# Skipping unused expert slots and moving expert choice, last down weights and result scatter in a one-core hybrid decoder layer

## The reference, cut to what matters

```python
x = layer_norm(DEEPNORM_ALPHA * x + mix, ln1_g, ln1_b)            # x1, (1024, 1024)
aff = sigmoid(x2 @ router_w)                                      # (1024, 32)
sel = aff + router_bias
grp_score = top_k(sel.reshape(N, 4, 8), 2)[0].sum(-1)
top_grp = argmax(grp_score, axis=-1)
_, idx = top_k(where(in_grp, sel, -inf), 2)                       # two experts of the best group
w_sel = take_along_axis(aff, idx, axis=-1)
gate = w_sel / sum(w_sel)
# each expert e, in blocks of 128 tokens:
h = silu(xblk @ w_gate[e]) * (xblk @ w_up[e])                     # 1024 x 512 each
y = h @ w_down[e]                                                 # 512 x 1024
x = layer_norm(DEEPNORM_ALPHA * x + sum of the two y * gate, ln2_g, ln2_b)
```

## Time and profile before

| | us |
|---|---|
| median of 3 runs | 2498.57 |
| lowest and highest | 2492.93, 2500.19 |
| the profiled execution | 2487.82 |
| its span, first to last instruction | 2486.0 |
| PE busy | 2225.8 (90%) |
| DVE busy | 1279.5 (51%) |
| ACT busy | 890.7 (36%) |
| POOL busy | 577.1 (23%) |
| granted TensorE clock, mean | 0.953 of full speed |

### The profile page before, as it was taken

How to read it: one execution, slowest core, us unless ns; L and a number is a source line. 1 busy time by engine, 2 the same in 40 slices (tenths; PEclk the granted TensorE clock), 3 DMA queues, 4 the chain that set the end, 5 groups by cost and what they waited for, 6 DMA issues and landing times. The chain is left out here.

```text
span 2486.0 us, 31375 instructions
## 1 busy us (share of the span) xinstructions
PE 2225.8 (90%) x12070; PEld 1789.7 (72%) x12071; DVE 1279.5 (51%) x1347; ACT 890.7 (36%) x846; POOL 577.1 (23%) x405
## 2 busy tenths in 40 slices
PE   6999799997899998989979889989489999999985
PEld 5667577774687787878867767868377877787762
DVE  2567421115130565236657701245578888888855
ACT  2653111114011343102224312011257777777753
POOL 2223211101240000424536522400011222121202
PEclk8999899999999999999989989989599999999998
DMA  3245423323531431422323231131389999999975
GB/s 119 88 138 166 149 80 101 96 56 106 198 119 37 112 78 33 154 101 94 110 81 105 87 110 43 60 121 68 135 315 387 394 391 383 389 406 378 390 306 211
DMA packets 125374, 428.48 MB, mean 172 GB/s; under 512 B 33424, under 2 KB 54800, under 8 KB 112352
## 3 DMA queue, kind: packets, MB, share of 16 engines
q1 hardware_dynamic: 106544, 354.29, 40.5%
q10 hardware_dynamic: 9136, 38.80, 3.9%
q0 software_dynamic: 9600, 34.08, 3.7%
HBM read 351.44 MB, written 75.69 MB: 172 GB/s over the span
## 5 line engine op out<-in xcount | busy, mean ns | idle before, releaser
L3045 DVE TENSOR_TENSOR ex_sb_low<-landed,high 128x4096 fp32r<-128x4096 f32 x96 | 424.6, 4424 | 121.6 <-ACT high L2986 117.1
L2986 ACT CAST high<-landed 128x4096 fp32r<-128x4096 f32 x93 | 337.7, 3632 | 114.7 <-DMA landed<-exp_gate 63.7
L2902 POOL COPY ex_sb_idx<-slot_token 128x1 uint32 x30 | 62.2, 2072 | 409.0 <-PE ex_ps_x L2924 409.0
L160 PE MATMUL ex_ps_g<-high,ex_sb_xt 128*128 128x512 f32 x256 | 105.8, 413 | 10.3 <-DVE ex_sb_xt L3040 10.2
L160 PE MATMUL ex_ps_y<-high,ex_sb_ht 128*128 128x512 f32 x256 | 104.3, 407 | 9.8 <-DVE ex_sb_ht L3057 9.8
L161 PE MATMUL ex_ps_g<-ex_sb_low,ex_sb_xt 128*128 128x512 f32 x256 | 102.8, 402 | 0.0
L1087 DVE TENSOR_TENSOR rc_sb_ab<-rc_ps_m,mats 128x512 f32<-128x512 f32 x32 | 20.6, 686 | 159.7 <-PE rc_ps_m L970 159.7
L162 PE MATMUL ex_ps_g<-high,ex_sb_xt 128*128 128x512 f32 x256 | 102.7, 401 | 0.0
L160 PE MATMUL ex_ps_u<-high,ex_sb_xt 128*128 128x512 f32 x256 | 101.3, 396 | 1.1 <-DVE ex_sb_low L3045 1.1
L161 PE MATMUL ex_ps_y<-ex_sb_low,ex_sb_ht 128*128 128x512 f32 x256 | 101.5, 396 | 0.0
L162 PE MATMUL ex_ps_y<-high,ex_sb_ht 128*128 128x512 f32 x256 | 101.5, 396 | 0.0
(11 more groups left out here) (549 smaller groups left out, 5863.5 us busy)
## 6 DMA issues: line engine op xcount, KB each, us to landing
landed<-exp_gate SPq DMA_DIRECT2D x31, 2048.0 KB, 10.6
landed<-exp_up SPq DMA_DIRECT2D x31, 2048.0 KB
landed<-exp_down SPq DMA_DIRECT2D x31, 2048.0 KB
y_slots<-ex_sb_y ACTq DMA_DIRECT2D x32, 512.0 KB, 11.5
chunk_ch<-slab SPq DMA_DIRECT2D x4, 2048.0 KB, 7.4
merged_d<-room SPq DMA_DIRECT2D x16, 512.0 KB, 2.9
room<-merged_d ACTq DMA_DIRECT2D x2, 4096.0 KB, 14.1
mixer_oT<-ssm_c SPq DMA_DIRECT2D x16, 512.0 KB, 4.0
```

The source lines that it names most:

```text
L160: nc.tensor.matmul(out, lhs[0], rhs[0], start=start, stop=False)
L2902: nc.gpsimd.tensor_copy(idx[b][:, :], k.slot_token[:, bass.ds(e, 1)]).then_inc(idx_ready, 1)
L2986: nc.scalar.copy(high[part][:, :], k.landed[part][:, :]).then_inc(high_ready[part], 1)
L3045: nc.vector.tensor_tensor(low[part][:, :], k.landed[part][:, :], high[part][:, :], ALU.subtract).then_inc(low_ready[part], 1)
```

## The change

- In `ssm_inputs` the zeroing of the overflow blocks is gone.
- In `out_project` the last tiles are reordered: the affinities of tiles 0 to 5 are made ahead, the choice of experts (a new function `choose_experts`, the same instructions as before over a range of tiles) runs on DVE for tiles 0 to 5 between the norms of tiles 6 and 7, and for tiles 6 and 7 at the end. ACT makes the affinities of tiles 6 and 7 directly from PSUM. PE runs 18 products that nobody reads ahead of the last turn.
- `route` begins with the slots. It now lists for each slot its token and its result row (choice x 1024 + token) in one product; unused slots get 1024 and 2048, which are past the bounds. The rounding of expert 0's down part moves to `experts`; POOL clears the two gather buffers; PE runs 6 unread products.
- In `experts` the gather takes its row numbers straight from the table and skips rows out of bounds; the store by ACT is replaced by a scatter from POOL to `k.y_rows` (row = choice and token), behind the gather of the expert four later in POOL's order, also skipping. The last down part goes to landing buffer 0, its rounded part to `high[0]`, its products to the PSUM tiles of gate and up, and DVE and ACT copy one half each. PE runs 14 unread products at the start.
- In `combine` the 16 gathers are plain loads from SP, and PE runs 16 unread products at the start.

The diff, cut to its core:

```diff
@@ ssm_inputs
-                    for n in range(OVER // (NCONV // 2 - 1)):
-                        for h in range(2):
-                            pool.dma_start(blocks[bass.ds(i * (OVER // (NCONV // 2 - 1)) + (E + n), 1), :, h * HALF:(h + 1) * HALF
-                                                  ].rearrange("a p d -> (a p) d"), zeros[:, 0:HALF]).then_inc(slots_zeroed, 16)
...
-                pool.wait_ge(slots_zeroed, 16 * 2 * OVER)
@@ out_project, PE
+                mix(NT - 2, 0)
+                turn(NT - 3, 1)
+                logits(NT - 4, 0)
+                logits(NT - 3, 1)
+                mix(NT - 1, 1, (0,))
+                turn(NT - 2, 0)
+                mix(NT - 1, 1, (1,))
+                logits(NT - 2, 0)
+                pe.wait_ge(mixed, NT + 1)
+                for n in range(IDLE_PRODUCTS):
+                    mm(ps[0][:, n % 2, :], high[1][:, n % KD, :], w_high[:, n % KD, 0:HALF], start=True, stop=True)
                 turn(NT - 1, 1)
-                logits(NT - 2, 0)
                 logits(NT - 1, 1)
@@ out_project, ACT
+                out_of_psum(NT - 3, 1)
+                root(NT - 2)
+                keep_logits(NT - 4, 0)
+                keep_logits(NT - 3, 1)
+                act.wait_ge(logits_copied, NT)
+                nc.scalar.activation(k.aff[:, 0:NT - 2, :], k.aff[:, 0:NT - 2, :], ACT.Sigmoid).then_inc(aff_ready, 1)
+                nc.scalar.activation(warm[:, :], eps[:, :], ACT.Sqrt).then_inc(table_in, 1)
+                out_of_psum(NT - 2, 0)
+                root(NT - 1)
...
+                affinity(NT - 2, 0)
                 out_of_psum(NT - 1, 1)
+                affinity(NT - 1, 1)
@@ out_project, DVE
+                picking(v.tensor_copy(grids[0][:, :, :], experts))
+                norm(NT - 2, 0)
+                dve.wait_ge(aff_ready, 1)
+                choose_experts(nc, k, picking, b_r, grids, rows, 0, NT - 2)
+                norm(NT - 1, 1)
+                dve.wait_ge(aff_ready, 3)
+                choose_experts(nc, k, picking, b_r, grids, rows, NT - 2, NT)
@@ route
+                link(ts(fold[:, :], listed_rows, float(T - UNUSED), float(-T), ALU.is_ge, ALU.mult))
+                v.scalar_tensor_tensor(k.slot_token[:, :], listed_rows, float(UNUSED), fold[:, :], ALU.add, ALU.add).then_inc(done, 1)
+                ts(k.slot_row[:, :], listed_rows, float(UNUSED), None, ALU.add).then_inc(done, 1)
@@ experts, SP
+                sp.wait_ge(low_ready[0], E)
+                load_expert(sp, k, E - 1, 2, LAST_DOWN)
@@ experts, POOL
+                def gather(e):
+                    pool.wait_ge(x_turned, e + 1)
+                    pool.indirect_dma_start(xb[e % 2][:, :], None, k.x1_d, bass.IndirectOffsetOnAxis(
+                        ap=k.slot_token[:, e:e + 1], axis=0), bounds_check=T - 1, oob_is_err=False).then_inc(x_in[e % 2], 16)
+                def scatter(e):
+                    if e >= 1:
+                        pool.wait_ge(y_out[(e - 1) % 2], 16 * ((e - 1) // 2) + 16)
+                        pool.sem_inc(y_free, 1)
+                    if e < E - 1:
+                        pool.wait_ge(y_kept, e + 2)
+                    else:
+                        pool.wait_ge(last_kept, 2)
+                    pool.indirect_dma_start(k.y_rows, bass.IndirectOffsetOnAxis(ap=k.slot_row[:, e:e + 1], axis=0),
+                                            y[e % 2][:, :], None, bounds_check=2 * T - 1, oob_is_err=False
+                                            ).then_inc(y_out[e % 2], 16)
+                for e in range(2, E):
+                    gather(e)
+                    if e >= 4:
+                        scatter(e - 4)
+                for e in range(E - 4, E):
+                    scatter(e)
@@ experts, PE
+                pe.wait_ge(low_ready[LAST_DOWN], E + 1)
+                pe.wait_ge(last_h_ready, 1)
+                for half, ps in ((0, ps_g), (1, ps_u)):
+                    for c in range(FF):
+                        m = product(E - 1, 1, LAST_DOWN, ps[:, :], last_ht, c, c * D + half * HALF, FF)
+                    m.then_inc(last_done, 1)
@@ experts, ACT
-                    act.dma_start(y_blocks[bass.ds(e, 1)].rearrange("a p d -> (a p) d"), y[b][:, :]).then_inc(y_out[b], 16)
@@ experts, DVE
-                dve.wait_ge(x_in[0], 16)
+                dve.wait_ge(first_issued, 1)
@@ combine
+                for t in range(NT):
+                    for n, y in ((0, y1), (1, y2)):
+                        sp.dma_start(y[:, t, :], k.y_rows[n * T + t * P:n * T + (t + 1) * P, :]).then_inc(y_in[t], 16)
-                        pool.indirect_dma_start(y[:, t, :], None, k.y_slots, bass.IndirectOffsetOnAxis(
-                            ap=k.dest[:, t, n:n + 1], axis=0)).then_inc(y_in[t], 16)
```

More of the change, by code:

```diff
@@ L2489, in out_project @@
         warm, table_in = s.sb("warm", [P, 1]), s.sem("table_in")
+        grids = [s.sb(n, [P, NT, E]) for n in ("idx_of", "cand", "eq")]
+        rows = [s.sb(n, [P, NT * EG]) for n in ("best", "first", "score", "g1")]
+        picks, IDLE_PRODUCTS = s.sem("picks"), 18
         ps = [s.ps(f"t{b}", [P, 2, HALF]) for b in range(2)]
@@ L2709, in route @@
         ps_rank, ps_count, ps_slots = s.ps("rank", [P, NT, E]), s.ps("count", [P, HALF]), s.ps("slots", [P, HALF])
-        (last, picked, counted, ranked, listed, slots_done, high_done, done) = (s.sem(n) for n in (
-            "last", "picked", "counted", "ranked", "listed", "slots_done", "high_done", "done"))
+        ps_idle, IDLE_PRODUCTS = s.ps("idle", [P, HALF]), 6
+        (last, picked, counted, ranked, listed, slots_done, high_done, done, cleared) = (s.sem(n) for n in (
+            "last", "picked", "counted", "ranked", "listed", "slots_done", "high_done", "done", "cleared"))
         with s.block() as block:
@@ L2760, in _ @@
                 m.then_inc(picked, 1)
-                link(ts(token[:, :], mat(k, "slot0", NT), mat(k, "row0", 1), None, ALU.add))
+                for j in range(2):
+                    link(ts(token[:, j], mat(k, "slot0", NT), mat(k, "row0", 1), float(j * T - UNUSED), ALU.add, ALU.add))
                 link(v.memset(one_e[:, :], 1.0))
@@ L2810, in _ @@
                 mm(ps_rank[:, :, :], mat(k, "ones"), before[:, 0:NT, :], start=False, stop=True).then_inc(ranked, 1)
+                for n in range(IDLE_PRODUCTS):
+                    mm(ps_idle[:, :], mat(k, "ident"), k.mats[:, 0:HALF], start=True, stop=True)
                 for j in range(2):
@@ L2816, in _ @@
                 m.then_inc(slots_done, 1)
+            @block.gpsimd
+            def _(pool):
+                for b in range(2):
+                    nc.gpsimd.memset(k.xb[b][:, :], 0.0).then_inc(cleared, 1)
+                pool.wait_ge(cleared, 2)
             @block.scalar
@@ L2950, in down @@
                     m.then_inc(used[2], 1)
+                for n in range(IDLE_AT_HEAD):
+                    nc.tensor.matmul(ps_y[:, n % 2, :], high[n % 2][:, 0:P], high[n % 2][:, 0:HALF], start=True, stop=True)
                 turn_x(0, 0)
@@ L2966, in _ @@
                 gate_up(E - 1, 1)
-                down(E - 2, 0)
-                turn_h(E - 1, 1)
-                down(E - 1, 1)
+                pe.wait_ge(low_ready[2], E - 1)
+                pe.wait_ge(h_low_ready, E)
+                pe.wait_ge(y_kept, E - 1)
+                for half in range(2):
+                    for c in range(FF):
+                        m = product(E - 2, 0, 2, ps_y[:, half, :], ht, c, c * D + half * HALF, FF)
+                    if half == 0:
+                        turn_h(E - 1, 1)
+                m.then_inc(used[2], 1)
+                pe.wait_ge(low_ready[LAST_DOWN], E + 1)
+                pe.wait_ge(last_h_ready, 1)
+                for half, ps in ((0, ps_g), (1, ps_u)):
+                    for c in range(FF):
+                        m = product(E - 1, 1, LAST_DOWN, ps[:, :], last_ht, c, c * D + half * HALF, FF)
+                    m.then_inc(last_done, 1)
             @block.scalar
@@ L2974, in _ @@
                 act.sem_inc(y_kept, 1)
-                for b in range(2):
-                    act.sem_inc(y_out[b], 16)
                 def high_x(e):
@@ L2999, in keep_y @@
                     act.wait_ge(used[2], e + 2)
-                    act.wait_ge(y_out[b], (e - b) * 8 + 16)
+                    act.wait_ge(y_free, e + 1)
                     nc.scalar.copy(y[b][:, :], ps_y[:, :, :].rearrange("p a b -> p (a b)")).then_inc(y_kept, 1)
-                    act.wait_ge(y_kept, e + 2)
-                    act.dma_start(y_blocks[bass.ds(e, 1)].rearrange("a p d -> (a p) d"), y[b][:, :]).then_inc(y_out[b], 16)
-                for part in range(3):
+                for part in range(2):
                     act.sem_inc(high_ready[part], 1)
+                act.wait_ge(k.landing[2], 16)
+                nc.scalar.copy(high[2][:, :], k.landed[2][:, :]).then_inc(high_ready[2], 1)
                 high_x(0)
@@ L3389, in trunk @@
         with ExitStack() as landing:
```

(2 more changed lines are left out.)

230 lines of the change are left out of this document (114 added, 116 removed).

## The result

The changed kernel takes **2459.64 us** (median of 4 runs, 2453.55 to 2470.72) beside 2495.75 for the kernel before (4 runs, 2491.56 to 2500.19): a ratio of 0.986, 95% interval 0.9824 to 0.9896. A second set, taken later, gave 2461.53 (4 runs, 2458.95 to 2465.61) and 0.9863 (0.9832 to 0.9894). The forecast was 2458, the range 2442 to 2480.

The account below looks back on a forecast made before the run. In the expert loop DMA sets the mean of 18.81 us an expert, PE only 3% under it; outside it, chains bind. Six terms sum to -40.2 us, set on the median of 2498.57: 2458 us, range 2442 to 2480.

Parts of the forecast that it names:

- Term 2: End of projection and routing: choosing experts for six tiles early shortens the chain to the picks; -6.1 us.
- Term 3: Head of the expert loop: first gate product 1.4 us earlier, and the warm PE does its products faster; -3.3 us.
- Term 5: Start of the combine: plain loads and filler products bring the first join at 9 to 11 us; -4 us.
- Term 1: Expert loop: skipping unused rows cuts traffic, so an expert takes 18.25 us instead of 18.81; -16 us.
- the ring: Expert loop: each weight part's cycle of landing (10.6 us), ACT's rounding (3.63) and DVE's subtraction (4.42), then the next issue; 18.7 us.
- PE's floor: Expert loop: PE's own time for an expert without waits, taken as 18.18 us.
- Term 4: Tail of the expert loop: earlier last down part, no PE wait, combine 31 us after gate 31; -10.8 us.
- (d): Expert loop: scatters, each waiting for the one before to land, set the period if over 18.2 us; 2523 us, chance 0.03.
- Term 6: State space inputs: removing the zeroing DMAs gains 0, at most -1 us, as PE is busy there.
- (a): Expert loop: skipped rows still take their time on the queues, so Term 1 is 0; 2474 us, chance 0.14.
- (b): Expert loop: scattered rows lower bandwidth, DMA still binds at 18.6 us or more; 2468 us, chance 0.10.
- (c): Projection, loop head, combine: fillers and moved parts collide; Terms 2, 3, 5 give 3 instead of 13.4; 2468 us, chance 0.10.

Follow-up runs that it names:

- e8: The kernel before, with every on-chip buffer of the expert stage at the address it has in the changed kernel; 2486.74 us.
- e3: The changed kernel, but the scatter of expert 31 does not wait until that of expert 30 has landed; 2438.31 us, a single run.
- e4: The changed kernel, with the waits for the last two scatters at the end of the expert stage on SP instead of POOL; 2449.68 us.
- e5: The changed kernel, with the 30 zeroing DMAs and the clearing of their source put back, written to a tensor nobody reads; 2467.13 us.
- e7: The changed kernel with the edits of e3 and e4 together; 2452.88 us, ratio 0.9865 to the kernel before.
- e13: The kernel of e7 again, timed beside the changed kernel on one chip; 2454.27 us, ratio 0.9846 to the kernel before.
- e1: The changed kernel with unused rows moved again: gathers read row 1023, scatters write to 128 spare rows; 2460.61 us.
- e12: The changed kernel with unused rows gathered and stored again, a second execution of e1; 2472.56 us.

## Why the prediction was right, step by step

The time was right to 2 us, and three terms of six hit; the other three missed by -5.5, +4 and +8.5 and partly cancelled. That the time came so near is luck in part: the medians fell by 36.1 us where I had 40.2, and the kernel before came out 2.8 under the 2498.57 that the forecast stands on.

**Term 2, the choice of experts: right**, -6.1 as forecast. The six-tile choice took 10.3 us as worked out, the last norm began 2.3 late against 3.1, from its start to the affinities were 10.9 against 10.2, the choice for two tiles took 7.2 against 7.3. To hit the sum to 0.1 is luck: from the projection's start to the experts' start the three kernels with the old order took 158.3 to 158.9 us and the eleven with the new one 152.0 to 154.1, 5.0 less by the means.

**Term 3, head: right in kind**, -4.4 against -3.3. The first gate product came 9.44 us into the stage (9.7 forecast). Of the 1.1 more, 0.3 lie there and 0.8 between gate 0 and gate 2. The faster matmuls can make the latter: e8, the kernel before at the new addresses, took 38.6 us from gate 0 to gate 2 instead of 39.95, in one execution.

**Term 5, combine: right**, -4.8 against -4. The first join starts 9.1 us in, at the short end of 9 to 11; the 16 filler products took 5.50.

**Term 1, loop: right in direction, mis-sized**, -13.0 over seven profiles against -16. The step that failed is the ring's: less backlog should bring the landing from 10.6 to 10.1 or less, and I put the mean near PE's floor of 18.18. The landing fell only to 10.3, since the weight packets themselves took 3% longer, and the ring of 18.35 sets the mean. The floor I took for fixed fell to 17.75 for a reason outside my list, the addresses. So bytes gave 6.9 where I wrote 16, and 6.1 came from what I did not count: about 1 between before and e8, some 5 unexplained, and both within the spread of single executions.

**Term 4, tail: mis-sized**, -2.3 in the pair, -10.8 forecast. PE's part was right to 0.5: y complete at +24.35 in the profile of after and +23.4 in e3, e4, e5, e7 and e13, against +23.9. The step that failed is "the scatter is issued like the store", with 0.9 for POOL's issue. I had named the scatters' order (each waits for the one before) in rival (d), for the loop, and not applied it to the last pair, where scatter 30 is issued at 2392.47, 3.74 us before the copy of the last half begins. And I took over 5.9 us from an ACT store for a POOL scatter, which takes 11.5: POOL's DRAIN of 5.28 us behind its last DMA was in no term. e7 and e13 show the sizes: without the first, and with 2.4 of the second's 5.6 gone, the combine begins at 33.3, where I had 31.

**Term 6, zeroing: wrong**, -5.5 against 0. I read 30 us in the middle, found PE busy for 29.13 of them, and took that for the stage. Neither the three PE waits elsewhere nor the stage's end, where POOL holds the barrier with a DRAIN of 2.51 us, is in that row. What a removed DMA of POOL is worth has to be looked for at the barrier that closes its stage, too.

**The rivals.** (a), skipped rows cost as much, falls: 6.9 us in e1 and e12. (b), DMA still binds, is half true: the weights' arrival still sets the period, at 18.4 and not above 18.6, and the rate did fall, from 388 to 369 GB/s (369 times 18.41 us is the expert's 6.8 MB). e12 moved 392 GB/s, so the 358 that the Trainium skill gives for a core's share (DMA: Bandwidth & Descriptors, Bandwidth; each core of a pair gets about that when both stream) did not limit this one core. (c), fillers collide, falls for Terms 2 and 5. In the head PE turned x at 1798.08, right behind 14 fillers of 0.42 us, at a granted clock of 0.54 from 1792 to 1798. The gathered rows had landed at 1797.20 (issued at 1792.77), so the fillers cost up to 0.9 us there. (d), the scatters set the period, falls in the loop: they land in 13.7 us there, under 18.2. But its mechanism is what ate Term 4.

## What to carry to other kernels

Where transfers go round a ring of load, convert, subtract, a byte saved is worth only what it takes off the landing time: here skipping took 7% of the bytes and 1.3% of the loop (539.5 to 532.6). When a store is replaced by an indirect one, price its end and not only its issue, above all for the last one of a stage: who waits for it, what it waits for itself, and the DRAIN of POOL behind it. And before calling an edit free because an engine is busy, read the stretch to the barrier that closes the stage, instructions of the sequencers included.

## What the runs showed of the hardware

**POOL's indirect DMA stands still while DVE subtracts.** In the loop of the kernel after, 52 of 57 such issues took 3.05 to 5.04 us instead of 0.97, and each of these 52 ended 0.86 to 0.90 us behind the end of a subtraction with two on-chip inputs. None of the five short ones began inside a subtraction. One pair, POOL ends at 2039.77 and DVE at 2038.89:

```profile
2034.46 4.43 DVE L3117 TENSOR_TENSOR ex_sb_low<-landed,high 128x4096 fp32r<-128x4096 f32 x1 [2.52 <-ACT high L3056]
...
2034.74 5.03 POOL L2939 DMA_INDIRECT xb<-x_d,slot_token  x1 [7.39 <-PE ex_ps_x L2982]
```

The Trainium skill, GPSIMD Engine Reference, Key points, has contention in this case; the rows show a wait to the end. No wait of PE or ACT in the loop names POOL, so it cost nothing that shows.

**Addresses change the matmul's pace**: 0.233 to 0.227 us from matmul to matmul, 18.18 to 17.75 for an expert, with the same matmuls and shapes, at a granted clock of 0.99 to 1.00. e8 shows it; which address does it no run shows.

**A skipped row is still a packet**, under 512 bytes. On queue 0 some 3650 of them in place of full rows of 4 KB took the time share from 13.6 to 7.3%, about as the bytes fell (29.80 to 14.87 MB).

**POOL's DRAIN, at the end of a stage in which it issued DMAs, took microseconds**: 2.51 us with the plain zeroing DMAs and under 0.5 without them, 5.28 behind the scatter, or 5.29 counted from the end of the scatter's issue where it follows at once. It is an instruction of the sequencer, so that no view of busy time shows it. Why it takes 2.51 in one case and 5.28 in the other no run shows, nor what the tail gains if the last store of the stage goes out from another engine.
